# Queries and gates of a gated recurrence as half-size products, both directions in one block, two tiles away in DRAM meanwhile

## The reference

```python
proj = h @ w_in[l]
z, xbc, dt_raw, q, f_fwd, f_bwd, i, g = jnp.split(proj, IN_SPLITS, axis=-1)
y_ssd = ssd_mixer(z, xbc, dt_raw, ...)
y_hg = hgrn2_mixer(q, f_fwd, f_bwd, i, g, lower_bounds[:, l], hg_norm_w[l])
y = jnp.concatenate([y_ssd, y_hg], axis=-1).astype(x.dtype) @ w_out[l]
x = x + gate1 * y
```

## Time and profile before

| | |
|---|---|
| median of 3 runs | 3675.73 us (3672.73 to 3681.72) |
| the profiled execution | 3674.47 us |
| its span, first to last instruction | 3672.7 us |
| mean granted clock of TensorE | 0.952 |
| `hgrn_inputs`, TensorE's first product to the next block's | 2633.88 to 2922.88 us |
| first direction of the recurrence, then the second, to the next block's first product | 2922.88, 3025.37, 3123.34 us |

### The profile page before, as it was taken

How to read it: one execution, slowest core, us unless ns; L and a number is a source line. 1 busy time by engine, 2 the same in 40 slices (tenths; PEclk the granted TensorE clock), 3 DMA queues, 4 the chain that set the end, 5 groups by cost and what they waited for, 6 DMA issues and landing times. The chain is left out here.

```text
span 3672.7 us, 35084 instructions
## 1 busy us (share of the span) xinstructions
PE 3399.4 (93%) x12610; PEld 1909.9 (52%) x12610; DVE 1599.3 (44%) x2814; ACT 772.6 (21%) x1570; POOL 266.8 (7%) x373
## 2 busy tenths in 40 slices
PE   8995689999988899999999999698999989989998
PEld 3443338444554344444444444235544589768886
DVE  6883725983353111111111111466526288644554
ACT  2103211122121101101101001225444256220001
POOL 1000021000001000000000000100000187000000
PEclk9995699999998999999999999799999999999999
DMA  8860037211136999999999996513323110312220
GB/s 267 291 207 30 7 149 280 72 69 66 69 124 250 406 404 389 399 404 385 401 396 395 400 393 250 201 47 93 119 93 113 35 30 30 137 51 88 92 92 24
DMA packets 209097, 711.44 MB, mean 194 GB/s; under 512 B 16198, under 2 KB 27544, under 8 KB 174156
## 3 DMA queue, kind: packets, MB, share of 16 engines
q1 hardware_dynamic: 183436, 633.45, 45.7%
q0 software_dynamic: 14576, 48.71, 3.8%
q10 hardware_dynamic: 10960, 27.63, 2.0%
HBM read 655.86 MB, written 53.89 MB: 193 GB/s over the span
## 5 line engine op out<-in xcount | busy, mean ns | idle before, releaser
L2533 PE MATMUL bank<-moe_gu,all_hT 128*128 128x512 f32 x1088 | 469.9, 592 | 3.1 <-PEq L2201 1.9
L2730 DVE TENSOR_SCALAR all_hT<-bank 128x512 f32<-128x512 f32 x51 | 35.3, 691 | 813.9 <-PE bank L2539 668.3
L2533 PEld LDWEIGHTS bank<-moe_gu,all_hT 128*128 128x128 f32 x1088 | 206.6, 190 | 262.9 <-issue 261.5
L2553 PE MATMUL bank<-moe_gu,all_hT 128*64 128x512 f32 x1088 | 238.2, 596 | 1.5 <-DVE all_hT L2731 1.5
L2573 PE MATMUL bank<-moe_dn,moe_rows 128*128 128x512 f32 x512 | 224.0, 595 | 3.9 <-ACT moe_rows L2652 3.9
L1919 PE MATMUL bank<-all_hT,early_w 128*128 128x512 f32 x512 | 220.2, 592 | 0.0
L2553 PEld LDWEIGHTS bank<-moe_gu,all_hT 128*64 128x64 f32 x1088 | 80.8, 138 | 156.0 <-issue 153.7
L1919 PEld LDWEIGHTS bank<-all_hT,early_w 128*128 128x128 f32 x512 | 97.3, 190 | 122.0 <-issue 122.0
L2573 PEld LDWEIGHTS bank<-moe_dn,moe_rows 128*128 128x128 f32 x512 | 96.0, 190 | 122.5 <-issue 114.8
L1981 DVE SCALAR_TENSOR_TENSOR b_conv<-conv_ya,all_table,b_conv 128x512 f32<-128x512 f32 x240 | 159.4, 744 | 0.0
L3750 PE MATMUL bank<-hg_qs,hg_ks 128*128 128x64 f32 x896 | 118.1, 285 | 25.1 <-ACT hg_ks L3653 14.0
(11 more groups left out here) (779 smaller groups left out, 5424.1 us busy)
## 6 DMA issues: line engine op xcount, KB each, us to landing
moe_gu<-in_w_gu_dram SPq DMA_DIRECT2D x136, 2048.0 KB, 14.4
moe_dn<-in_w_dn_dram SPq DMA_DIRECT2D x68, 2048.0 KB, 13.9
early_w<-in_w_in_dram SPq DMA_DIRECT2D x13, 2048.0 KB, 9.1
expert_rows<-b_z POOLq DMA_DIRECT2D x49, 512.0 KB, 20.3
mods_w<-in_w_mod_dram SPq DMA_DIRECT2D x48, 512.0 KB, 5.3
mods_w<-in_ada_w_dram SPq DMA_DIRECT2D x48, 512.0 KB, 4.9
late_w<-in_w_up_dram SPq DMA_DIRECT2D x8, 2048.0 KB, 9.0
late_w<-in_w_down_dram SPq DMA_DIRECT2D x8, 2048.0 KB, 7.7
```

Source lines behind the costliest of these rows:

```text
L2533: mm = nc.tensor.matmul(B[bank][:], xb2[:, k, :], gu[:, q, kk, col:col + HALF], start=(k == 0), stop=False)
L2553: mm = nc.tensor.matmul(B[bank][part, :], xb1[:, k % 4, k // 4, :], gu[:, 4 + q, kk, col + h * HALF:col + (h + 1) * HALF], start=(k == 0), ...
L2730: vec.tensor_scalar(g, gate[:], SWIGLU_LIMIT, None, ALU.min).then_inc(clipped, 1)
```

## The change

Queries and gates are made as eight steps of two tiles by `SevenProducts`, the first step whole, the other seven of seven half-size products. The sums lie where `xT` and `y_ssd` were: both go to DRAM in the block (`x_away` from SP's queue at its start, `y_away` from POOL's queue after the norm) and come back during the recurrence, on SP's queue ahead of the kept rows of passes 3 and 4. The gates get their Silu in a separate ScalarE step, in place. `hgrn_direction`, called twice, becomes `hgrn_recurrence`, one block of 16 passes; the masks of both directions are loaded at its start, cut to the columns that are used; `A` and `S` are cleared again where the direction changes. The first output weights are asked for some five passes earlier.

```diff
+    parts["levels"] = np.concatenate([a[:, c] for a, c in zip(levels, met)], 1)
...
 def hgrn_inputs(...)
+        units = [dict(src=hT, into=lambda n: q[:, n % KT, :]), dict(src=hT, into=lambda n: gate[:, n % KT, :])]
+        own = SevenProducts(core, ctx, stream, "hgate", units, (SevenProducts.weights_within(xT),
+                                                                *SevenProducts.parts_within(y_ssd[:, 6:8, :])),
+                            (SevenProducts.values_within(y_ssd[:, 0:6, :]),), eager=[1], whole=[0])
+        own.base, own.pieces = base + 3 * KT, stream.taken + 6
...
 sync
+            sp.dma_start(x_away, xT.rearrange("p k t -> p (k t)")).then_inc(x_stored, 16)
 gpsimd
+            pool.wait_ge(ssd_normed, KT)
+            pool.dma_start(y_away, y_ssd.rearrange("p k t -> p (k t)")).then_inc(core.y_ssd_stored, 16)
 tensor
-            for i in range(5):
+            for i in range(3):
...
+            for n in range(own.count):
+                if n < 2:
+                    pe.wait_ge(copied, 2 * KT + 4 * (n + 1))
+                if n in own.whole:
+                    own.multiply_whole(pe, n)
+                else:
+                    own.multiply(pe, n, own.order(n))
 scalar
-            for n in range(8):
-                act.wait_ge(done, n + 1)
-                take(QUERY, n, q[:, n, :], ACT.Identity)
-            for n in range(8):
-                act.wait_ge(joined, KT + n + 1)
-                take(GATE, n, gate[:, n, :], ACT.Silu)
...
+            act.wait_ge(done, 2)
+            own.whole_out(act, 0)
+            for n in range(1, own.count):
+                own.first_out(act, n)
+                act.wait_ge(done, min(2 * n + 2, KT))
+                own.corner_out(act, n)
+                if n > 4:
+                    open_gate(n - 1)
+            open_gate(own.count - 1)
 vector
             for d in range(2):
+                if d:
+                    dve.wait_ge(x_stored, 16)
+                    dve.wait_ge(core.y_ssd_stored, 16)
...
+                if d:
+                    own.weigh(dve, 1)
+                    for i in (0, 1, 3):
+                        own.add_values(dve, 0, i)
                 for k in range(KT):
...
+            own.weigh(dve, 2)
+            own.add_values(dve, 0, 2)
+            for n in range(1, own.count):
+                own.join_first(dve, n)
+                own.join_last(dve, n)
+                if n + 2 < own.count:
+                    own.weigh(dve, n + 2)
...
-def hgrn_direction(core, d, q, G, K, total, v_tm, y, ident, kept_dram, ahead):
+def hgrn_recurrence(core, q, sums, keys, totals, v_tm, y, ident, kept_dram, ahead, back):
+    PASSES = 2 * HG_H
...
+            for h in range(PASSES):
                 if h >= 2:
                     sp.wait_ge(product, NM * (h - 1))
+                if h in (3, 4):
+                    to, away = back[h - 3]
+                    sp.dma_start(to.rearrange("p k t -> p (k t)"), away).then_inc(brought_back, 16)
+                if h == HG_H + 2:
+                    ahead(sp)
...
-            vec.tensor_scalar(less[:], edges, -1.0, None, ALU.mult).then_inc(negated, 1)
+            for d in range(2):
+                vec.tensor_scalar(less[:, d], edges[d], -1.0, None, ALU.mult).then_inc(negated, 1)
...
+                if h in (HG_H, HG_H + 1) and j == 0:
+                    vec.memset(A[:, h % 2, :], 0.0).then_inc(started, 1)
+                    dve.wait_ge(started, 3 + h % 2)
...
-                keep = halves(mask[:, j, :], m)[:, :, q_half, :].bitcast(U32)
+                keep = close(mask[:, d, j * P // 2:(j + 1) * P // 2], m).bitcast(U32)
...
+                if h == HG_H:
+                    dve.wait_ge(out_made, h)
+                    vec.memset(S[:, order[0], :], 0.0).then_inc(cleared, 1)
+                    dve.wait_ge(cleared, 1)
```

More of the change, by code:

```diff
@@ L79, in constant_parts @@
               for m in (64, 32, 16, 8, 4, 2, 1)]
-    parts["levels"] = np.concatenate(levels + [row == col], 1)
-    parts["levels_back"] = np.concatenate([a.T for a in levels] + [row == col], 1)
+    met = [i[(i // m) % 2 == 1] for m in (64, 32, 16, 8, 4, 2, 1)]
+    met_back = [i[(i // m) % 2 == 0] for m in (64, 32, 16, 8, 4, 2, 1)]
+    parts["levels"] = np.concatenate([a[:, c] for a, c in zip(levels, met)], 1)
+    parts["levels_back"] = np.concatenate([a.T[:, c] for a, c in zip(levels, met_back)], 1)
     parts["block_number"] = row
@@ L3350, in hgrn_inputs @@
         (copied, loaded, diffed, magnitude, rate, log_term, kept, outer_magnitude, outer_rate, outer_term, log_sig,
-         kept_log, apart, joined, logged, summed, totalled, shifted, done) = sems(
+         kept_log, apart, joined, logged, summed, totalled, shifted, done, opened) = sems(
             nc, ctx, *(f"hgate_{s}" for s in (
@@ L3465, in _, with open_gate @@
                 take(VALUE, n, v_tm[:, n % 4, n // 4 * HALF:(n // 4 + 1) * HALF], ACT.Identity)
-            for n in range(8):
-                act.wait_ge(done, n + 1)
-                take(QUERY, n, q[:, n, :], ACT.Identity)
-            for n in range(8):
-                act.wait_ge(joined, KT + n + 1)
-                take(GATE, n, gate[:, n, :], ACT.Silu)
+            def open_gate(n):
+                own.joined(act, n)
+                for i in range(2):
+                    tile = own.units[n // 4]["into"](2 * n + i)
+                    func(tile, tile, ACT.Silu).then_inc(opened, 1)
+            act.wait_ge(done, 2)
[7 more added lines that the diff above has]
+            open_gate(own.count - 1)
         @block.vector
@@ L3534, in hgrn_direction @@
     NM = NL + 1
-    order = list(range(TT)) if d == 0 else list(range(TT))[::-1]
+    orders = (list(range(TT)), list(range(TT))[::-1])
+    PASSES = 2 * HG_H
     R = 4
@@ L3768, in _ @@
             pe.wait_ge(zeroed, 1)
-            for h in range(HG_H):
+            for h in range(PASSES):
+                head = h % HG_H
                 for i in range(NL):
@@ L3794, in _ @@
                 pe.wait_ge(kept_loaded[h % 2], 16 * (h // 2 + 1))
-                pairs(h, NL, q[:, h, :], kept[:, h % 2, :])
-            output(HG_H - 1)
+                pairs(h, NL, q[:, head, :], kept[:, h % 2, :])
+            output(PASSES - 1)
 def mixed_out(core, stream, first_w, first_loaded, y, y_ssd, y_hg, gain, gate, ones, scratch, spare, xT, scale):
```

135 lines of the change are left out of this document (75 added, 60 removed).

## The result

The changed kernel takes 3692.52 us, median of 5 runs (3691.18 to 3694.38), against 3675.73 before (5 runs, 3672.73 to 3681.72): a ratio of 1.0045, 95% interval 1.003 to 1.0059. It is slower by 16.8 us; the forecast was 3691, that is +16.2 on the profiled execution. The profiled execution has a span of 3690.7 us.

The account below looks back on a forecast made before the run. TensorE, busy 93% of the span, was taken as the bound. Terms 25.6 + 1.0 + 0.4 − 11.3 + 0.5 gave +16.2 on 3674.5 us, 3690.7; with the median's 1.3 above, forecast 3691 us, range 3680 to 3699.

Parts of the forecast that it names:

- The stop at product 7: Input block, step 1: TensorE idles 20 to 24 us for value sum t3, queued behind VectorE's second loop and weigh(2).
- the cover: Input block before the change: TensorE's uninterrupted products hide the ScalarE and VectorE chain, claimed only 5 us longer than it.
- Rival 1: Input block: no wait at product 7 if t3 comes by 2826; gain of 11.6 us stands, 3653.5 us; chance 6%.
- The restart: Input block, after the long pause: the clock restarts at half, costing 2.0 us, between bounds 1.4 and 3.1.
- the input term: Queries and gates: TensorE ends at 2942.8 instead of 2917.2, pause and slow clock included, +25.6 us.
- Tail and start: Last gate tile waits for another addition and Silu, +1.0 us; two less operations open the recurrence, +0.4 us.
- One block for both directions: Recurrence: the change of direction becomes an ordinary pass, −11.3 us; second clearings of A and S cost +0.5.
- Away and back: Residual and state-space result, 2 MB each, leave to DRAM and return before passes 3 and 4: hidden, price 0.
- masks: Recurrence: mask reads without gaps don't speed the picks, price 0; other bound 0.70 us less per pass.
- rival 2: Recurrence: gapless masks shorten the narrow picks, about 0.5 us a pass counts, 7.5 us less, 3683.5 us; chance 18%.
- Rival 3: Clock stays low longer or a refill takes half the turn's gain: 3 to 6 us more, 3694 to 3698; chance 14%.
- The point named as deciding: End of VectorE's second loop in the input block: at about 2841 instead of 2857.6 the change is neutral, earlier it gains.

Follow-up runs that it names:

- joins in the loop: Changed kernel with value sum t3 ahead of VectorE's second backward loop, joins of steps 1, 2 and weight sums of 3, 4 spread through its turns: 3669.87 us.
- queries whole: Changed kernel with the four query steps as whole products, only gate steps as seven products, value copies early: 3657.81 us, 0.9956 of before.
- sum early: Changed kernel with weigh(2) and add_values(0, 2), the sum for product 7 of step 1, moved ahead of VectorE's second backward loop: 3683.87 us.

## Why the prediction was right

**The stop at product 7.** As written: step 0 of 13.7 us, a pause, fragments, then a pause of 24.05 us (20 to 24 foretold) that ends with `t3` behind `weigh(2)`. From the block's first product to product 7 the prediction has 54.0 us (2861.4 − 2807.37) and the trace 53.97 (2865.09 − 2811.12). One reading ahead of it doesn't hold: the cover is not only 5 us longer than VectorE's loop. Before the change the first gate tile, at 2862.30, needs only the first query copy, which ends at 2829.72 on ScalarE, so the loop could have come some 30 us later. No term of the sum uses the 5 us. Rival 1, no stop, is out. Its price was wrong too: it takes the undisturbed gain of 11.6 us, although the same text has step 1 waiting 8.1 us for the value copies whatever `t3` does. In the kernel with the joins in the loop, where the long stop is gone, the block is 4.7 us longer than before and not 10 shorter, so an early `t3` would not have brought 3653.5.

**The restart.** Behind the stop the granted clock is 0.57 for 6.12 us. The first two products take 3.54 and 2.58 us from start to start where 1.73 is usual: 2.66 us lost, not the 2.0 taken. This is nearly the whole miss of the input term, 26.2 measured (136.08 − 109.87) for 25.6. It lies inside the bounds of 1.4 and 3.1.

**Tail and start.** +1.0 and +0.4 were taken for the gap ahead of the recurrence; it grew from 5.64 to 6.66 us (2953.86 − 2947.20), +1.02, which is the tail alone. The second `less` operation starts 0.11 us behind the first and ends with it (its rows stand with the narrow picks), so its price is at the lower bound.

**One block for both directions.** −11.3 for the turn came as 11.28. With the clearings the recurrence was to give −10.8 and gave −11.7. The two passes in which A is cleared take 11.49 us each, 0.12 more than an ordinary one, half of the 0.5 taken; against before even that is made up, since the pass behind the turn took 11.59 there. The other 0.5 us of the gain lies at the start, from the recurrence's first product to the diagonal product of its second pass: 24.16 us (2978.02 − 2953.86) where before it took 24.63 (2947.51 − 2922.88). The sum has no term for it, and its cause is not shown.

**Away and back, masks.** Both priced at 0, both measured at 0. For the way back it is 188.73 against 188.72 us; on the way out TensorE has no stop, being busy for 173.97 of the 174.02 us from 2637.10 to the first query product. The masks leave a pair at 1.56 us, so rival 2 falls. Its price was sound: with gapless writes, not reads, a pair does give 0.46 us a pass, about the 0.5 that it named. By the Trainium skill (SBUF — State Buffer, section Door 1: The DMA port swizzle) each step to a new line of 16 bytes costs. The mask's reads here don't show it: half as many steps, the same 1.56 us. The writes into A go with it: runs of 2 and 1 elements with gaps cost 0.56 us more a pair than without. But the same paragraph of the Trainium skill takes two accesses to a line as enough for full bandwidth, and these writes make two, so the rule doesn't settle what costs.

**The sum** was +16.2; the two stretches measure +15.5, the medians +16.8. The stretches are the test of the steps. That the median came within 1.5 us of 3691 is in part luck: in the profiles the unchanged code ahead of the block took 3.75 us more and that behind the stretches 1.2 us less. Rival 3, a longer shadow, didn't come: the clock behind the long stop was back within two products, and the turn's gain came in full. That was not certain: the same recurrence lost some 3.6 us to the lower clock in two of the experiments (the last section).

The point named as deciding, VectorE's loop, stands: with the joins in its turns the change is about neutral, with TensorE covered until it ends (queries whole) the change gains.

## What to carry to other kernels

A form that saves products but needs sums from another engine is only as early as the place of these sums in that engine's queue: look first at what the helper is doing in that stretch, here a loop of 33 us that TensorE's eight ordinary query tiles used to cover. Moving one late operation ahead only uncovers the next one behind the same loop; either all of them go among its turns, or the new form is used only where the loop is over. When a change has two parts of opposite sign, run each alone, and measure stretches between two marks of one engine rather than totals.

## What was not expected of the hardware

The clock behind one and the same pause of 6.5 us ahead of the recurrence came back at different times. In the changed kernel it was 1.00 from 2966.00 on, 12 us after the first product (2953.86):

```profile
2953.86:2960.00 6.14, 6.14 (x30) 6.14 (x30) 4.14 (x8) 3.27 (x9) 6.14 (x8) 0.50 0.01 5
2960.00:2966.00 6.00, 6.00 (x31) 6.00 (x30) 2.52 (x6) 4.91 (x16) 3.63 (x6) 0.51 0.01 3
2966.00:2972.00 6.00, 5.54 (x50) 5.43 (x50) 5.69 (x11) 3.02 (x8) 5.49 (x8) 1.00 0.19 46
```

With the queries whole it took 18 us (windows from the recurrence's first product on, and then that of pass 8 to 9):

```profile
2914.96:2921.00 6.04, 6.04 (x29) 6.04 (x30) 4.14 (x8) 3.27 (x9) 6.04 (x8) 0.50 0.02 6
...
2927.00:2933.00 6.00, 6.00 (x32) 6.00 (x32) 3.84 (x9) 2.39 (x6) 2.60 (x5) 0.54 0.08 15
2933.00:2939.00 6.00, 6.00 (x56) 6.00 (x56) 4.18 (x11) 2.82 (x9) 4.98 (x7) 1.00 0.08 30
...
3020.66:3033.80 13.14, 12.03 (x94) 11.92 (x94) 10.71 (x22) 7.72 (x24) 10.09 (x15) 0.87 0.30 101
```

The same kernel drops to 0.87 in the pass after the turn, behind a wait of 1.11 us that the changed kernel has too (1.09 us) without a drop; the pass takes 13.14 us instead of 11.49. The kernel with the sum early shows both (its pass takes 13.12 us), the one with the joins in the loop only the late return, for 1.9 us. Together they make the 3.7 us that the recurrence with the queries whole takes longer than in the changed kernel (192.40 − 188.72). What decides was not tried and stays open; with one profile for each kernel it is not even shown whether it belongs to the kernel or to the single execution.
